# Moving the operands of the three-pass matmuls onto multiples of 1024 bytes

## The reference, cut to what matters

```python
# first_block, for i in (0, 1)
q, k, v = jnp.split(x @ w_qkv, 3, axis=-1)              # differential attention, i = 0
qkv = (x @ w_qkv).reshape(B, S, G, 3, H, E)             # dilated attention, 3 groups, i = 1
...
q = (x @ w_q).reshape(B, S, H, E)                       # cross attention
kv = (mem @ w_kv).reshape(B, M, 2, H, E)
gate, val = jnp.split(x @ w_in, 2, axis=-1)             # conv GLU, hidden 2816
...
return (jax.nn.gelu(gate, approximate=False) * val) @ w_out
# second_block: modulation, a Mamba-2 mixer (context, then latent), SwiGLU,
# a conformer convolution module, SwiGLU
mod = sc @ w + b                                        # six shift/scale/gate vectors
zxbcdt = h @ w_in
return (jax.nn.silu(u[..., :FFN_HIDDEN]) * u[..., FFN_HIDDEN:]) @ w_out
```

## Time and profile before

| | |
|---|---|
| median of 3 runs | 2066.23 us (2062.2 to 2067.2) |
| the profiled execution | 2065.53 us; its span in the trace 2063.8 us |
| TensorE matmul busy | 1916.5 us, 93% of the span, 13629 matmuls |
| TensorE weight loads busy | 1696.5 us, 82% |
| GpSimd busy | 1255.1 us, 61% |
| VectorE, ScalarE busy | 1090.8 us (53%), 999.2 us (48%) |
| HBM read | 339.65 MB, 165 GB/s over the span |
| mean granted TensorE clock | 0.969 of full |

### The profile page before, as it was taken

One profiled execution on the slowest core, in us unless ns is written; L12 is line 12 of the kernel. 1 busy time (PEld: TensorE's weight loads), 2 busy tenths in 40 slices (PEclk: granted clock), 3 DMA queues, 4 the chain that ended last, 5 costly groups with the idle time before them and its releaser, 6 DMA issues.

```text
span 2063.8 us, 34083 instructions
## 1 busy us (share of the span) xinstructions
PE 1916.5 (93%) x13629; PEld 1696.5 (82%) x13629; DVE 1090.8 (53%) x1524; ACT 999.2 (48%) x1726; POOL 1255.1 (61%) x583
## 2 busy tenths in 40 slices
PE   7989999998999989989999899898879999998997
PEld 7879788887999866868887788876669987968996
DVE  5473346633610173146667655688665623856981
ACT  4654345543444473435553444378735545625542
POOL 8767566786888405546788334200468886426995
PEclk9999999998999999999999899999989999999999
DMA  6435367864555405358763212221235553324552
GB/s 261 142 142 184 112 259 305 319 258 153 198 190 184 143 1 194 136 216 304 311 250 143 82 64 100 82 82 62 83 132 183 183 184 143 123 82 153 189 194 106
DMA packets 49217, 342.30 MB, mean 166 GB/s; under 512 B 5264, under 2 KB 7312, under 8 KB 8144
## 3 DMA queue, kind: packets, MB, share of 16 engines
q1 hardware_dynamic: 47440, 331.02, 43.6%
q0 software_dynamic: 1664, 9.70, 1.2%
HBM read 339.65 MB, written 1.05 MB: 165 GB/s over the span
## 4 chain that ended last, share of the span: by engine, by line
PE 70%; DVE 14%; ACT 6%; POOL 6%; issue 2%; DMA 2%; DVEq 0%; SPq 0%; ACTq 0%; POOLq 0%
PE bank L1724 13%; PE bank L1726 12%; PE bank L1728 12%; PE bank L1779 10%; POOL w_lo L2232 4%; PE bank L1954 2%; PE bank L1829 2%; PE bank L1326 2%; PE bank L1328 2%; PE bank L1329 2%; PE bank L1756 2%; PE bank L1759 2%; PE bank L1758 2%; DMA ring<-slabs_dram 2%; ACT wh_area L1160 2%
## 5 line engine op out<-in xcount | busy, mean ns | idle before, releaser
L2232 POOL TENSOR_TENSOR w_lo<-ring,w_hi 128x1024 fp32r<-128x1024 f32 x360 | 876.7, 2462 | 287.7 <-ACT w_hi L2821 287.2
L1724 PE MATMUL bank<-x_hi,w_hi 128*128 128x256 f32 x2176 | 616.5, 283 | 18.1 <-POOL w_lo L2232 14.3
L1728 PE MATMUL bank<-x_lo,w_hi 128*128 128x256 f32 x2176 | 610.0, 280 | 0.0
L2821 ACT ACTIVATE w_hi<-ring 128x1024 fp32r<-128x1024 f32 x448 | 448.8, 1052 | 326.1 <-DMA ring<-slabs_dram 319.4
L1724 PEld LDWEIGHTS bank<-x_hi,w_hi 128*128 128x128 f32 x2176 | 417.5, 192 | 38.2 <-issue 36.7
L1728 PEld LDWEIGHTS bank<-x_lo,w_hi 128*128 128x128 f32 x2176 | 413.9, 190 | 0.0
L1726 PE MATMUL bank<-x_hi,w_lo 128*128 128x256 f32 x1472 | 413.4, 281 | 0.0
L1726 PEld LDWEIGHTS bank<-x_hi,w_lo 128*128 128x128 f32 x1472 | 280.9, 191 | 0.0
L2232 POOL TENSOR_TENSOR w_hi<-ring,w_hi 128x1024 fp32r<-128x1024 f32 x88 | 209.0, 2396 | 99.9 <-ACT w_hi L2821 99.9
L2745 ACT ACTIVATE arena<-bank 128x512 f32<-128x512 f32 (+1 forms) x144 | 80.0, 559 | 274.5 <-PE bank L1728 191.0
L1726 PE MATMUL bank<-x_hi,w_hi 128*128 128x256 f32 x704 | 197.1, 280 | 0.0
(11 more groups left out here) (360 smaller groups left out, 3689.0 us busy)
## 6 DMA issues: line engine op xcount, KB each, us to landing
ring<-slabs_dram SPq DMA_DIRECT2D x308, 1024.0 KB, 4.8
lnrow<-ln_dram POOLq DMA_DIRECT2D x6, 1024.0 KB, 5.0
arena<-slabs_dram SPq DMA_DIRECT2D x4, 1024.0 KB, 7.9
xt<-xT_dram SPq DMA_DIRECT2D x1, 1024.0 KB, 5.7
xt<-memT_dram SPq DMA_DIRECT2D x1, 1024.0 KB, 11.9
x<-x_dram SPq DMA_DIRECT2D x1, 1024.0 KB, 13.6
arena<-ctx_dram POOLq DMA_DIRECT2D x1, 1024.0 KB, 7.7
lnrow<-ln_dram POOLq DMA_DIRECT2D x2, 512.0 KB, 4.7
```

What stands on the lines that cost most here:

```text
L1724: ins = pe.matmul(dst, wh[:, k, c], src[0][:, k, :], start=(k == 0), stop=False)
L1728: ins = pe.matmul(dst, wh[:, k, c], src[1][:, k, :], start=False, stop=(k == KC - 1))
L2232: pool.tensor_tensor(dst[:, c], ring[:, s, c], w_hi[:, s, c].bitcast(F32), ALU.subtract).then_inc(S["lo_ready"], 1)
L2821: a.activation(w_hi[:, g % RING, c], ring[:, g % RING, c], ACT.Copy) \
```

## The change

It moves tensors in SBUF. No instruction is added or removed, none changes its engine, its place in the order, its shape or its waits.

```diff
+        small = sb("small", [P, 480])
         xh_at = aligned()
+        assert xh_at % 1024 == 0
         xh_area = sb("xh_area", [P, 2048])
 ...
         row = sb("row", [P, NROW])
-        small = sb("small", [P, 576])
-        mod = sb("mod", [P, 2, 6, 8, 2])
+        pick_area = sb("pick_area", [P, 32])
         sc_in = sb("sc_in", [P, KC, 32])
         xlat = sb("xlat", [P, KC, T])
+        sb("rest", [P, 16])
         xt2_at = aligned()
+        assert xt2_at % 1024 == 0
         xt2 = sb("xt2", [P, KC, 2 * T])
 ...
         ring = sb("ring", [P, RING, SLAB])
+        mod = sb("mod", [P, 2, 6, 8, 2])
 ...
-        pick = small[:, 264:296]
-        modA = small[:, 168:184]
-        lamp = small[:, 312:440]
-        dtn = small[:, 312:568].rearrange("p (t h) -> p t h", t=4)
-        epsb = small[:, 568:569]
+        pick = pick_area[:, :]
+        modA = small[:, 152:168]
+        lamp = small[:, 216:344]
+        dtn = small[:, 216:472].rearrange("p (t h) -> p t h", t=4)
+        epsb = small[:, 472:473]
```

More of the change, by code:

```diff
@@ L263, in build @@
         half16 = small[:, 136:152]
-        pick = small[:, 264:296]
-        modA = small[:, 168:184]
-        lamp = small[:, 312:440]
-        dtn = small[:, 312:568].rearrange("p (t h) -> p t h", t=4)
-        epsb = small[:, 568:569]
[L269 to L276, removed]
+        pick = pick_area[:, :]
[3 more added lines that the diff above has]
+        epsb = small[:, 472:473]
+        sub_col = small[:, 198:199]
+        qscale = small[:, 168:176]
+        tok_i = small[:, 176:184].bitcast(I32)
+        tok_f = small[:, 184:190]
+        sq = small[:, 190:194].rearrange("p (s t) -> p s t", s=2)
+        var2 = small[:, 194:196]
+        rstd2 = small[:, 196:198]
+        dcol = small[:, 200:216]
         qT = cut(0, 8, T)
@@ L383, in build @@
         pair_sum = part("pair_sum", place(28480, 64), 64)
-        sq4 = small[:, 206:210]
+        sq4 = small[:, 190:194]
         uraw = cut(0, 8, 512)
```

## The result

| | before | after |
|---|---|---|
| median | 2065.95 us (4 runs, 2062.2 to 2067.2) | 2092.07 us (4 runs, 2090.45 to 2095.49) |
| profiled execution, its span | 2065.53, 2063.8 us | 2095.49, 2093.8 us |

The ratio is 1.0134, with a 95% interval of 1.0117 to 1.0151: the change makes the kernel 1.3% slower. The forecast was 2045, with a range up to 2078.

A forecast was written before the change was run, and what follows sets the result against it. TensorE's own matmul rate was taken as the bound. Savings of about 17 us over 256 columns and 6.2 us over 512 made 23 us, cut 10% to 21, giving a median of 2045 us; range 2010 to 2078.

The forecast's parts named there:

- That addresses matter, by their relation: TensorE's two operands: equal byte offsets are the cheap case, by 2.4 to 9 ns a 512-column matmul.
- The 512-column terms: Row stage, mixer and L1548 over 512 columns: equal offsets save 3.1, 2.4 and 0.7 us, together 6.2 us.
- the mixer's: L1326, L1328 and L1329 over 512 columns: 480 matmuls save 5 ns each, 2.4 us.
- L1548's: The mixer's last product: 192 matmuls save 3.6 ns each, 0.7 us.
- The 256-column terms: All 256-column groups: slow matmuls reach the fast 113.3 ns, saving 8.1, 4.6 and 4.3 us, about 17 us.
- The slow one: Rival: equal offsets lock the slow rate in 256- and 512-column matmuls; 2086, up to 2094 us; chance 0.17.
- its point of decision: Dilated attention projections, 512 to 707 us: the slow rival holds if they run at 118 ns throughout.
- Much faster by absolute alignment: Rival: three-pass matmuls on multiples of 1024 gain 60 to 90 us, 1975 to 2005; chance 0.14, including part-way below 2035.
- Nothing happens: Rival: a stretch's beginning picks the rate, so the mix stays; 2065 us within 6; chance 0.23.
- the windows: Dense 256-column stretches: should show one rate, some 600 matmuls in 68 us for 580, 1094 in 124 us for 1047.

The follow-up runs named there:

- e1_all128: The changed kernel with small widened by 32 columns, so every three-pass matmul operand lies 128 bytes over a multiple of 1024; 2092.31 us.
- e2_x128_w960: The changed kernel's tensor order with the offsets of the kernel before, x group at 128 and weight group at 960; 2062.6 us, 0.9993 of before.

## Why the prediction was wrong

**What bounds the kernel.** Right. The time moved with PE's rate alone, 32 us of busy time and 30 us of span, and no other engine took part.

**That addresses matter, by their relation.** Right, and against the rule of the Trainium skill's "SBUF — State Buffer", section "Who interferes with whom", that PE waits for nobody and its two read ports are independent: by it the sum was 0, and the measured one is 26 us between medians. What the page says of other engines the trace bears out: a step took 119.8 ns with all of them idle and 119.9 with all busy. For which two reads meet see the 512-column trace above; for 256 columns it stays open.

**The 512-column terms.** Right in sign and nearly in size. I put equal offsets at 226.7 ns from the earlier trace rows; the row stage came to 227.1, the mixer's projection to 228.2. The terms gave 6.2 us, measured 4.6; the mixer's gave 5 ns a matmul and measured 3.5, L1548's 3.6 and 1.9.

**The 256-column terms.** This is the step that failed: "since the fast rate there is exactly half of 226.7, I take it that equal offsets also end in the fast rate". That 113.3 is half of 226.7 says at most that both forms share a lowest rate, and nothing on who reaches it. Equal offsets gave 120.0, 6.7 above the fast rate; before, no stretch of the two main 256-column forms ran at it. A reason may be that at 256 columns a load of 128 columns has to be done within each stream and at 512 has twice the time, so that the same collision costs one form and not the other; no run shows this. Where I had -17 us stands +38.

**What I had and did not use.** The earlier trace rows show L1328, which streams s_hi past an equal w_half, and I quoted them for the rival and then weighed more. The 256-column part of the same lines, near 1310 us, has steps of 114, 118 and 121 ns, the 118 being the equal pair by R1: the nearest steps to the case in width as well as in relation. Nor are the earlier trace rows the one place where the relation changes while all else stays, as I wrote; the earlier trace rows are such a place. And the same relation cost 235 ns in the earlier trace rows and 229 in the earlier trace rows, which should have warned me that a rate does not go with a pair alone. Rows of 512 columns were carried over to a term of 256 columns that weighs three times as much in my own sum.

**The rivals.** The slow one was right in direction and place: equal offsets lock one slow rate, and its point of decision, the projections of the dilated attention at one rate throughout, is what the first window above shows. That its 2086 to 2094 holds the 2092 is partly luck, since two sizes in it were off and nearly cancelled: the rate is 120.0 and not 117.7, and the 512-column matmuls gained instead of losing. Its reason, two streams that meet at their first read, was not shown. I gave it 0.17. Much faster by absolute alignment fell with the result, where no form came below its fast rate of before, and e1_all128 shows that the multiple of 1024 does nothing by itself. What the Trainium skill's "TensorE: Matmul & The Clock Gate", section "Back-to-back issue gap", gives as N / 2.4 + 2.5 ns is the gap of an isolated matmul, which I had used for a stream; no stream of 256 columns in any run came to its 109.2. "Nothing happens" failed with the windows.

**The range.** It should have held the whole of the slow rival, since no row showed 256 columns at equal offsets for long, and the trace had pairs that spoke each way.

## What to carry to other kernels

In a dense stream of float32r matmuls read the distance between starts, not the shown duration: a few ns a matmul were 1.3% of this kernel's time. If that distance sits on two or more fixed values with nothing else changed, suspect the placement of the operands in SBUF, and try shifts of 32 or 64 bytes between streamed and kept tensors, each form by itself. Don't align both to the same round number without measuring: here it was the worst place for 256 columns (level with a difference of 96 where the weights stream) and the best for 512.

## What the runs showed of the hardware

- Three-pass float32r matmuls with 128x128 kept operands, at a granted clock of 1.00, run at a rate that goes by the relation of the two operands' byte addresses modulo 256. Over 256 columns the x-streaming form has a mean of 119.9 ns a step at a difference of 0, 115.2 at 64 and between 117.3 and 118.8 at 32, 96, 128 and 192. Over 512 columns the row stage has 227.1 at 0, 229.0 at 64 and 232.9 to 233.4 at the others.
- At 64 bytes two rates, 113.3 and 117.7 ns, exist side by side for the same lines and addresses, each kept over stretches of 100 us and more.
- Plain float32 matmuls are not slowed: L1829 takes 0.430 us a step with operands at 960 and 128 and the same, 0.43, with both at 0 in the changed kernel.
- In the x-streaming form moving w_lo alone by 64 bytes changed all three steps of a group, from 120.0 to 117.6, 118.3 and 117.6 (h1_lo64). In L1548, over 512 columns, moving one kept operand changed one step of six, from 235 to 227.
- VectorE was busy 1090.8 us before, 1025.7 after and 1138.2 in e2_x128_w960, with the same instructions; the time of e2 is that of before.
